# Forgetting attention: keys and queries of a head loaded side by side and turned in one pass, low queries on 64 rows, two head buffers used in turn

## The reference: what is computed

```python
def fox_prompt(q, k, v, logf):               # q, k, v: (1, 2048, 8 heads, 64)
    scale = Dh ** -0.5
    c = jnp.cumsum(logf, axis=1)
    ...
        s = jnp.einsum('bqhd,bkhd->bhqk', qi, k).astype(jnp.float32) * scale
        s = s + cqi[..., :, None] - ck[:, :, None, :]
        mask = kpos[None, :] <= qpos[:, None]
        p = jax.nn.softmax(jnp.where(mask, s, -jnp.inf), axis=-1)
        return jnp.einsum('bhqk,bkhd->bqhd', p.astype(v.dtype), v)
```

## Time and profile before

| | before |
|---|---|
| median of 3 runs | 2874.49 us (2866.94 to 2875.61) |
| the profiled execution, its own time | 2877.13 us |
| its span | 2875.3 us |
| mean granted clock of PE | 0.983 of full |
| PE busy | 2705.3 us (94%) |
| DVE, ACT, POOL busy | 1718.0, 1149.9, 1609.3 us |

### The profile page before, as it was taken

One profiled execution on the slowest core, in us unless ns is written; L12 is line 12 of the kernel. 1 busy time (PEld: TensorE's weight loads), 2 busy tenths in 40 slices (PEclk: granted clock), 3 DMA queues, 4 the chain that ended last, 5 costly groups with the idle time before them and its releaser, 6 DMA issues. The chain is left out here.

```text
span 2875.3 us, 42289 instructions
## 1 busy us (share of the span) xinstructions
PE 2705.3 (94%) x15137; PEld 2436.1 (85%) x15137; DVE 1718.0 (60%) x2246; ACT 1149.9 (40%) x1926; POOL 1609.3 (56%) x905
## 2 busy tenths in 40 slices
PE   8999989889889988799979999999999989999998
PEld 7998989777777777677879999999999977888887
DVE  5375686477787787676475657565756553224332
ACT  4212311466666667533343334333433332113221
POOL 3476688488979889465556666666655620000111
PEclk9999999899999999999989999999999999999999
DMA  6587889567666666676533323333256437445553
GB/s 210 174 274 244 272 261 305 149 165 186 175 176 174 185 169 187 177 238 196 186 123 118 105 92 124 126 104 118 79 118 144 102 97 216 132 132 165 164 162 109
DMA packets 483759, 476.76 MB, mean 166 GB/s; under 512 B 154952, under 2 KB 380035, under 8 KB 482519
## 3 DMA queue, kind: packets, MB, share of 16 engines
q1 hardware_dynamic: 464542, 451.95, 54.1%
q10 hardware_dynamic: 18720, 21.05, 2.1%
q0 software_dynamic: 288, 1.05, 0.1%
HBM read 392.83 MB, written 81.14 MB: 165 GB/s over the span
## 5 line engine op out<-in xcount | busy, mean ns | idle before, releaser
L2462 PE MATMUL ps_gate_up<-h_hi,w_hi 128*128 128x344 f32 (+1 forms) x1848 | 594.6, 322 | 26.6 <-DVE h_lo L2377 9.8
L2464 PE MATMUL ps_gate_up<-h_hi,w_lo 128*128 128x344 f32 (+1 forms) x1848 | 594.7, 322 | 0.0
L2463 PE MATMUL ps_gate_up<-h_lo,w_hi 128*128 128x344 f32 (+1 forms) x1848 | 594.2, 322 | 0.0
L2462 PEld LDWEIGHTS ps_gate_up<-h_hi,w_hi 128*128 128x128 f32 x1848 | 350.5, 190 | 30.6 <-issue 11.4
L2463 PEld LDWEIGHTS ps_gate_up<-h_lo,w_hi 128*128 128x128 f32 x1848 | 350.6, 190 | 0.0
L2464 PEld LDWEIGHTS ps_gate_up<-h_hi,w_lo 128*128 128x128 f32 x1848 | 350.6, 190 | 0.0
L867 PE MATMUL ps_proj<-w_hi,h_hi 128*128 128x428 f32 (+1 forms) x800 | 288.8, 361 | 10.7 <-ACT proj_out L591 10.6
L2744 PE MATMUL ps_down<-wd_hi,act_hi 128*128 128x512 f32 x704 | 275.8, 392 | 10.4 <-DVE wd_lo L2660 10.4
L868 PE MATMUL ps_proj<-w_lo,h_hi 128*128 128x428 f32 (+1 forms) x800 | 285.2, 357 | 0.0
L869 PE MATMUL ps_proj<-w_hi,h_lo 128*128 128x428 f32 (+1 forms) x800 | 284.6, 356 | 0.0
L1540 DVE TENSOR_TENSOR p_lo<-ps_turned,p_hi 128x512 fp32r<-128x512 f32 (+1 forms) x352 | 214.5, 616 | 110.8 <-ACT p_hi L1447 109.2
(11 more groups left out here) (320 smaller groups left out, 6355.0 us busy)
## 6 DMA issues: line engine op xcount, KB each, us to landing
stock<-in_cache_k SPq DMA_DIRECT2D x192, 256.0 KB, 3.4
common<-in_cache_v SPq DMA_DIRECT2D x172, 256.0 KB, 3.0
common<-in_w_gate SPq DMA_DIRECT2D x33, 1024.0 KB, 6.7
common<-in_w_up SPq DMA_DIRECT2D x33, 1024.0 KB, 6.0
stock<-out_proj SPq DMA_DIRECT2D x48, 512.0 KB, 7.4
stock<-act_turned SPq DMA_DIRECT2D x16, 1408.0 KB, 8.1
act_raw<-act_turned SPq DMA_DIRECT2D x16, 1408.0 KB, 8.1
page_v<-in_cache_v SPq DMA_DIRECT2D x84, 256.0 KB, 3.1
```

The lines of the kernel that those rows point to most:

```text
L2462: pe.matmul(acc, a_hi, h_hi[:, m, d, 0:n], start=d == 0, stop=False)
L2463: pe.matmul(acc, a_hi, h_lo[:, m, d, 0:n], start=False, stop=False)
L2464: mm = pe.matmul(acc, a_lo, h_hi[:, m, d, 0:n], start=False, stop=d == H - 1)
```

## The change

The keys and the queries of a fox head are loaded once each, side by side (keys in columns 0 to 63 of each tile, queries in 64 to 127), and one Turn ("kq") transposes both: keys arrive on rows 0 to 63 of the bank, queries on rows 64 to 127. ACT makes three copies of 64 rows (k_hi, and q_hi twice), DVE two operations of 64 rows (k_lo, q_lo). `q_lo` now has 64 rows, and its product goes over rows 0 to 63 of `k_st` (q_lo with k_hi; the product q_lo with k_lo is left out). Even heads load into `a.q`, odd heads into `a.k`. Memory heads keep their form.

```diff
+def load_fox(eng, raw, head, sems):
+    eng.dma_start(raw[:, :, 0, :], head.k.rearrange("(t p) d -> p t d", p=P)).then_inc(sems[1], 16)
+    eng.dma_start(raw[:, :, 1, :], head.q.rearrange("(t p) d -> p t d", p=P)).then_inc(sems[0], 16)
...
-                        load_head(sp, shared.q, shared.k, shared.v, first_head, (c.first_q, c.first_k, c.first_v))
+                        load_fox(sp, shared.q, first_head, (c.first_q, c.first_k))
+                        load_value(sp, shared.v, first_head, c.first_v)
...
-        return ([Turn(head, "k", 0), Turn(head, "k", 1)] + fox_pieces(head, range(QCH)) + [SplitV(head)] + fox_pieces(head, range(QCH, 2 * QCH)) +
-                [Turn(head, "k", 2), Turn(head, "q", 2)])
+        return ([Turn(head, "kq", 0), Turn(head, "kq", 1)] + fox_pieces(head, range(QCH)) + [SplitV(head)] + fox_pieces(head, range(QCH, 2 * QCH)) +
+                [Turn(head, "kq", 2)])
...
-        first = [Turn(h, "k", 3), Turn(h, "q", 3)]
-        early = [Turn(h + 1, "q", 0), Turn(h + 1, "q", 1)] if is_fox(h + 1) else []
+        first = [Turn(h, "kq", 3)]
...
-                    if head <= FH:
-                        sp.wait_ge(s.in_turned, turn_index[Turn(head - 1, "q", 3)] + 1)
-                        sp.wait_ge(s.in_turned, turn_index[Turn(head - 1, "k", 3)] + 1)
-                        sp.wait_ge(s.v_lo, split_index[head - 1] + 1)
+                    if 2 <= head < FH + 2:
+                        sp.wait_ge(s.in_turned, turn_index[Turn(head - 2, "kq", 3)] + 1)
...
                             pe.matmul(at, a.q_hi[:, i * P:(i + 1) * P], a.k_st[:, b0:b1], start=True, stop=False)
-                            mm = pe.matmul(at, a.q_lo[:, i * P:(i + 1) * P], a.k_st[:, b0:b1], start=False, stop=not diag)
+                            rows = slice(0, HD if is_fox(item.head) else P)
+                            mm = pe.matmul(at, a.q_lo[rows, i * P:(i + 1) * P], a.k_st[rows, b0:b1], start=False, stop=not diag)
...
+                            if item.side == "kq":
+                                cols = slice(item.j * BLK, (item.j + 1) * BLK)
+                                act.activation(a.k_st[0:HD, cols], src[0:HD], ACT.Copy).then_inc(s.k_hi, 1)
+                                act.activation(a.q_hi[HD:P, cols], src[HD:P], ACT.Copy, scale=SCALE)
+                                act.activation(a.q_hi[0:HD, cols], src[HD:P], ACT.Copy, scale=SCALE).then_inc(s.in_hi, 1)
...
+                            if item.side == "kq":
+                                cols = slice(item.j * BLK, (item.j + 1) * BLK)
+                                dve.wait_ge(s.k_hi, 4 * item.head + item.j + 1)
+                                dve.tensor_tensor(a.k_st[HD:P, cols], src[0:HD], a.k_st[0:HD, cols].bitcast(F32), ALU.subtract)
                             dve.wait_ge(s.in_hi, turn_index[item] + 1)
+                            if item.side == "kq":
+                                dve.scalar_tensor_tensor(out=a.q_lo[0:HD, cols], in0=src[HD:P], scalar=SCALE,
+                                                         in1=a.q_hi[HD:P, cols].bitcast(F32), op0=ALU.mult, op1=ALU.subtract).then_inc(s.in_lo, 1)
```

More of the change, by code:

```diff
@@ L968, in attention_phases @@
     heads = FH + MH
-    phases = [("lead", [], [Turn(0, "q", 0), Turn(0, "q", 1)] + lead_items(0), 3)]
+    phases = [("lead", [], lead_items(0), 3)]
     for h in range(heads):
@@ L980, in attention_phases @@
         phases.append(("first", split[0], middle[0:4] + first + middle[4:], 3))
-        phases.append(("second", split[1], fox_pieces(h, range(3 * QCH, 4 * QCH)) + early, 2))
+        phases.append(("second", split[1], fox_pieces(h, range(3 * QCH, 4 * QCH)), 2))
         phases.append(("third", split[2], lead, 3))
@@ L1147, in attend, with landed @@
                     take(("row", b), s.row_out, b + 1)
-            def in_value(head):
-                return 16 * ((head - 1) // 2 + 1) if head % 2 else 16 * (head // 2)
+            def landed(head, side):
+                return sum(16 if is_fox(h) or side == "v" else 32 for h in range(1, head + 1) if h % 2 == head % 2)
             def piece_ready(piece):
                 i = piece.rows[-1]
-                wanted = [Turn(piece.head, "q", i // 4)]
-                wanted += [Turn(piece.head, "k", j) for j in range((piece.p1 + BLK - 1) // BLK if is_fox(piece.head) else 1)]
-                return max(turn_index[t] for t in wanted) + 1
+                if is_fox(piece.head):
+                    return turn_index[Turn(piece.head, "kq", i // 4)] + 1
+                return max(turn_index[Turn(piece.head, "q", i // 4)], turn_index[Turn(piece.head, "k", 0)]) + 1
             def bank_release(piece):
@@ L1219, in _ @@
                     for item in items_at(n - 3):
-                        if isinstance(item, Turn) and item.side == "q" and item.j == 3:
+                        if isinstance(item, Turn) and item.side != "k" and item.j == 3:
                             head = item.head
@@ L1455, in _ @@
                             else:
-                                act.activation(a.q_hi[:, item.j * BLK:(item.j + 1) * BLK], src, ACT.Copy,
-                                               scale=SCALE if is_fox(item.head) else -SCALE).then_inc(s.in_hi, 1)
+                                act.activation(a.q_hi[:, item.j * BLK:(item.j + 1) * BLK], src, ACT.Copy, scale=-SCALE).then_inc(s.in_hi, 1)
                         elif isinstance(item, SplitV):
@@ L1460, in _ @@
                             if item.head:
-                                act.wait_ge(v_in[item.head % 2], in_value(item.head))
+                                act.wait_ge(v_in[item.head % 2], landed(item.head, "v"))
                             else:
@@ L1526, in _ @@
                                 cols = slice(item.j * BLK, (item.j + 1) * BLK)
-                                dve.scalar_tensor_tensor(out=a.q_lo[:, cols], in0=src, scalar=SCALE if is_fox(item.head) else -SCALE,
+                                dve.scalar_tensor_tensor(out=a.q_lo[:, cols], in0=src, scalar=-SCALE,
                                                          in1=a.q_hi[:, cols].bitcast(F32), op0=ALU.mult, op1=ALU.subtract).then_inc(s.in_lo, 1)
```

47 lines of the change are left out of this document (28 added, 19 removed).

## The result

The changed kernel takes 2979.6 us (median of 4, 2971.9 to 2982.2) against 2871.5 us (4 runs, 2866.9 to 2875.6): ratio 1.0373, 95% interval 1.0345 to 1.0400. It is 3.7% slower; forecast were 2955 us and 2.8%. The forecast case came, and 25 us more.

The account below looks back on a forecast made before the run. PE was taken to bound the kernel, busy 94% of the span, about 7 us idle per head. 2877.1 - 14 + 125 - 28 + 0 - 3 = 2957.1, less 2.6: about 2955 us, 2.8% slower; range for 8 in 10, 2850 to 2990.

Parts of the forecast that it names:

- The forecast case: q_lo's products on PE: late start and exposed weight load both paid at each change of shape; 2955 us, chance 0.62.
- Change of placement, +125: Low queries' 320 products on 64 rows: 640 changes of shape on PE at 0.20 us each, +125 us, bounds 0 and +128.
- idle time takes 28: PE's waits for DVE's score banks, ACT's exponentials and p_lo take up part of the added work: -28 us, bounds 0 and -45.
- Rival 1 (free): q_lo's products on PE: the change of shape costs nothing; about 2857 us, faster by 0.6%, chance 0.24.
- rival 2 (drain only): q_lo's products on PE: only 0.09 us per change is paid, loads still made ahead; about 2890 us, chance 0.10.
- Rival 3 (the granted clock): PE's clock falls in score slots because it pauses 80 times per head; about 55 us more, 3010 us, chance 0.04.
- Turns removed and start, -17: 32 groups of raw transposes leave PE, -14 us; fewer loads and Turns before the attention's first score, -3 us.
- ACT and DVE in a Turn, taken as 0: Three ACT copies of 64 rows replace two of 128, +19 us on ACT; taken as 0 because ACT has 21 us free per head.
- The bound of +19: Cost if p_hi queued behind a Turn's three ACT copies held PE each time: +19 us.
- Start, -3: Start of the attention: three loads and one Turn before the first score save barrier and chain, -3 us, bounds -1 and -5.
- The range of the forecast case: 2915 us (-45 taken up, 0.17 per change) to 2990 us (nothing taken up, half of the ACT term).

Follow-up runs that it names:

- grouped kernel: Changed kernel with a row's q_hi products first and its q_lo products behind them, 48 changes of placement per head instead of 80: 2930.0 us, ratio 1.0208.
- full placement: Changed kernel with q_lo's products on all 128 rows, q_lo's upper half made zero once in head 0: 2869.8 us, ratio 0.9990.
- 96 rows: Kernel before with the fox heads' q_lo product over rows 0 to 95: 2869.9 us, ratio 0.9999.
- two-copy kernel: Changed kernel with q_lo's products on 128 rows and the third ACT copy made in head 0 alone: 2859.1 us, ratio 0.9956.
- the moved Turn: Changed kernel with q_lo's products on 128 rows and a head's second Turn behind its first four score pieces: 2894.3 us, ratio 1.0084.
- the copy from SBUF: Changed kernel, q_lo's products on 128 rows; q_lo waits for the second copy alone, ACT's third reads SBUF instead of PSUM: 2874.5 us, ratio 1.0002.
- both together: Changed kernel, q_lo's products on 128 rows, third copy from SBUF and second Turn behind the first four score pieces: 2889.3 us, ratio 1.0047.
- before, with 64 rows: Kernel before with only the fox heads' q_lo product put on rows 0 to 63, Turns not halved: 2997.2 us, ratio 1.0438.
- the third copy on DVE and by DMA: Changed kernel, q_lo's products on 128 rows, third copy taken off ACT: by DVE 2899.2 us, ratio 1.0104; by DMA within SBUF 2899.6 us, ratio 1.0094.

## Why the prediction was right, and where its sizes were off

**Change of placement, +125, of which idle time takes 28: the mechanism as forecast.** Start to start at 512 columns is 0.43 us as worked out, 0.20 more than between full products. The timeline of the grouped kernel shows the split. There a full product stands behind a change (its load waits 0.37 us, "issue") and another full one behind it:

```profile
755.41 0.50 PE L1433 MATMUL ps_out<-p_hi,v_stacked 128*128 128x512 f32 x1
755.75 0.39 PE L1434 MATMUL ps_out<-p_lo,v_stacked 128*128 128x512 f32 x1
```

Here it is 0.34 us: 0.11 for the exposed load. The 0.09 that is left is the late start. Shorter blocks pay less: at 128 columns q_lo's product takes 0.26 us start to start (712.90 to 713.16) and 0.11 in the kernel before (678.23 to 678.34). PE is busy 73.2 to 73.5 us in a clean head against 416.93 / 7 = 59.6 with full placement (window 605.06 to 1076.69), so 13.7 us per head, 110 in all and not 125 (a few matmul records are missing in both). Idle time falls from 54.7 / 7 = 7.8 to 5.1 us per head, so 22 are taken up and not 28 (25 if the whole attention is counted: from 530 to 1320 us, PE's waits before the transposes of probabilities, q_hi's products, the value products, the raw transposes and the foldings sum to 82.0 us in full placement and 56.8 in the changed kernel). Net 88, forecast 97. The Trainium skill, "TensorEngine Tiling (Array Packing)", Tiling Modes, counts a contraction of 64 as another tiling mode and says that a change of mode drains the engine. The trace agrees in the late start of 0.09 us; 96 rows, which stay in the full placement, pay nothing.

**Rival 1 (free) and rival 2 (drain only) fell.** The loads are not made ahead, at 0.25 us of "issue" each. The Trainium skill, "TensorE: Matmul & The Clock Gate", Part 2, says that a weight load of 32 rows takes the time of one of 128. The trace agrees for 64 rows (loads of 0.18 and 0.19 us, products of 0.49 to 0.50 us for both), but this tells nothing of what a change between 64 and 128 costs.

**Rival 3 (the granted clock) was given 0.04 and 55 us as a case of its own; it came beside the forecast, at 20 us.** The argument against it, that pauses of 0.1 us are far shorter than waits that leave the clock at 1.00, did not rule it out. By the reckoning above the kernel before lost 14 us, full placement, the two-copy kernel and 96 rows 12 to 17, the moved Turn, the copy from SBUF and both together 18 to 23, the grouped kernel 25, and those with 64 rows throughout 33 (before, with 64 rows) to 38. The mean clock of the whole execution, which is on record for every run, says the same: 0.983 to 0.984 before (33 runs in all), 0.982 in full placement, 0.975 in the changed kernel, 0.973 in the kernel before with 64 rows. As an estimate, (1 - clock) times the time is 75 us in the changed kernel and 52 in full placement. But the placement is not needed for it. The kernels with the third copy on DVE and by DMA have no 64 rows and more waits; they lost 28 and 30 us by the windows, and their mean clock is 0.976. So it is an association. No run holds the pauses and changes the clock alone, and what brings the clock down stays open.

**Turns removed and start, -17: borne out for the kernel that was forecast** (17.6 us, from the kernel before with 64 rows to the changed one), **and not with full placement** (3 us; 12.6 with two copies). **ACT and DVE in a Turn, taken as 0, is the step whose reasoning failed.** It gave three copies "three slots before PE needs p_hi" and looked at p_hi alone. The copies took 0.58 to 0.60 us each as forecast; late behind them were q_lo, and so a bank, and the output bank's copy. Of these the step named none. In the changed kernel's own trace this is the 9.0 us for q_lo and the 10.7 for p_lo before the transposes. With full placement the third copy costs 10 us. What it costs in the changed kernel was not measured, and the 17.6 us leave little room for it. In both pairs the waits of PE, summed as above, rise by 4 us through the pairing (52.9 to 56.8, and 78.4 to 82.0); what differs is the clock, whose estimate falls from 82 to 75 us with 64 rows and rises from 46 to 52 with full placement. The bound of +19 held it.

**Start, -3: right where it was measured.** Timeline of PE at the start, kernel after:

```profile
547.22 1.42 PE L1370 MATMUL ps_turned<-ident,stock 128*128 128x128 f32 x8 [2.56 <-PEq L84]
550.48 0.47 PE L1384 MATMUL ps_scores<-k_stacked,q_hi 128*128 128x128 f32 x1 [1.84 <-DVE q_lo L1547]
```

PE waits 1.2 us less and needs 3.3 us to the first score instead of 5.6. That the attention began 3.6 us later comes from the stage before it, in which PE's last products ran later in this execution; why, the trace was not asked. Full placement began at 543.1.

**Sum with measured terms:** by way of full placement, -14 - 3 + 10 + 88 + 21 (38 - 17 of the clock) = +102, against 108 measured. By way of the kernel before with 64 rows it is +124 - 17.6 = +106; these two are differences of times and so must come near. The six us of the first are not accounted for; the clock of one execution and the spread of the medians are of that size. By either way the forecast came out low for one reason above all: the clock, which the forecast case put at nothing and which took about 20 us.

**The range of the forecast case** begins at 2915 "with 45 taken up, and 0.17 per change". Its own terms give 2877.1 - 14 + 109 - 45 - 3 - 2.6 = 2922. Nothing hangs on it: the range stated goes down to 2850.

No kernel that computes all of it beats the kernel before by what can be measured. The two-copy time, 2859 us, is what the pairing could give if the queries' second half came for nothing; no place for that copy was found.

## What to carry to other kernels

Before a contraction is cut from 128 to 64 rows to save weights or zeros, count how often it alternates with full ones: each change costs about 0.17 us here, the clock's part included, while 96 rows or a zeroed upper half cost nothing; if 64 rows are needed, put their products next to each other. When one pass replaces two on the bound engine, list everything that is queued on the copying engines behind its results, the banks' copies too, not only the operand that is needed next. An operation moved off a full engine is worth trying only where the next user has slack for its latency, and a copy within SBUF on DVE should be priced with what POOL runs beside it.

## What was not expected of the hardware

- A DVE copy within SBUF of 64 x 512 took 0.42 us with POOL idle and up to 3.18 us beside a POOL instruction, with its end 0.28 us behind that one's; the mean of 28 is 1318 ns. ACT took 630 ns for the same copy and 594 from PSUM.
- A busier PE did not keep its granted clock: 0.73 over the first 100 us of the changed kernel with PE busy 90%, against 0.91 in the kernel before at 81%. It fell as well in kernels that wait more and have no 64 rows (third copy on DVE, 0.97 over 640 to 1180 us), so neither the busy share nor the placement tells it alone. The kernel before:

```profile
540.00:640.00 100.00, 80.93 (x466) 66.34 (x466) 73.14 (x146) 65.36 (x124) 79.86 (x28) 0.91 0.68 176
```
